# Gated delta layer: heads two tiles earlier, gates as the fifth tile, and a recurrence and spreads in another form

## The reference, cut to what matters

```
proj = h @ w_in                       # 1024 x (4*1024 + 16)
qkv, z, beta_logit, a_logit = split(proj)
qkv = silu(causal_conv(qkv, w_conv))  # 4 taps
q = q * rsqrt(sum(q*q)) / sqrt(128);  k = k * rsqrt(sum(k*k))
beta = sigmoid(beta_logit);  g = -exp(a_log) * softplus(a_logit + dt_bias)
# per head, per chunk: L = strict(k_beta k^T * decay);  T = (I + L)^-1
# u = T v_beta;  w = T (k_beta exp(g));  qk = causal(q k^T * decay)
# scan over chunks:
v_new = u - w @ state
o = q_dec @ state + qk @ v_new
state = state * exp(g_last) + k_dec^T @ v_new
y = (rms_norm(o) * silu(z)) @ w_out
```

## Time and profile before

| | |
|---|---|
| runs | 2340.86, 2342.62, 2348.20 us |
| profiled execution | 2341.71 us, of which the span is 2339.90 us |
| mean granted TensorE clock | 0.966 |
| TensorE matmuls | 2211.8 us busy, 95% |
| VectorE / ScalarE / GpSimd | 1127.8 / 854.7 / 412.3 us (48 / 37 / 18%) |
| DMA | 182.12 MB, mean 78 GB/s |

### The profile page before, as it was taken

One profiled execution on the slowest core, in us unless ns is written; L12 is line 12 of the kernel. 1 busy time (PEld: TensorE's weight loads), 2 busy tenths in 40 slices (PEclk: granted clock), 3 DMA queues, 4 the chain that ended last, 5 costly groups with the idle time before them and its releaser, 6 DMA issues. The chain is left out here.

```text
span 2339.9 us, 29203 instructions
## 1 busy us (share of the span) xinstructions
PE 2211.8 (95%) x10830; PEld 1776.7 (76%) x10830; DVE 1127.8 (48%) x1805; ACT 854.7 (37%) x1405; POOL 412.3 (18%) x459
## 2 busy tenths in 40 slices
PE   7999999999889999998899999999999997899989
PEld 6888887666677888887788878886777886776657
DVE  5444324423436444324575543346565775655433
ACT  4322223443334322223432241135445753433453
POOL 2111003112423111001210010002100241014441
PEclk8999999999989999999999999999999996999999
DMA  4333333411022333331333256740242220233202
GB/s 135 116 93 96 95 97 84 95 45 55 19 72 72 108 97 94 97 94 50 109 90 99 72 91 97 101 72 1 72 119 74 68 58 10 73 86 73 48 18 70
DMA packets 359321, 182.12 MB, mean 78 GB/s; under 512 B 41925, under 2 KB 356014, under 8 KB 358830
## 3 DMA queue, kind: packets, MB, share of 16 engines
q1 hardware_dynamic: 359214, 180.69, 31.0%
HBM read 176.14 MB, written 4.52 MB: 77 GB/s over the span
## 5 line engine op out<-in xcount | busy, mean ns | idle before, releaser
L313 PE MATMUL ps<-xh,wh 128*128 128x512 f32 x1920 | 766.0, 399 | 10.8 <-DVE wl L280 4.2
L315 PE MATMUL ps<-xh,wl 128*128 128x512 f32 x1920 | 749.3, 390 | 0.0
L314 PE MATMUL ps<-xl,wh 128*128 128x512 f32 x1920 | 748.5, 390 | 0.0
L280 DVE TENSOR_TENSOR wl<-raw,wh 128x1024 fp32r<-128x1024 f32 x334 | 422.6, 1266 | 435.7 <-ACT wh L270 431.0
L270 ACT ACTIVATE wh<-raw 128x1024 fp32r<-128x1024 f32 x334 | 342.1, 1027 | 375.3 <-PE ps L315 332.1
L313 PEld LDWEIGHTS ps<-xh,wh 128*128 128x128 f32 x1920 | 360.9, 188 | 102.9 <-issue 22.2
L315 PEld LDWEIGHTS ps<-xh,wl 128*128 128x128 f32 x1920 | 360.7, 188 | 77.3
L314 PEld LDWEIGHTS ps<-xl,wh 128*128 128x128 f32 x1920 | 361.1, 188 | 73.0 <-issue 2.4
L458 PE MATMUL ps<-xh,wh 128*128 128x512 f32 x304 | 129.9, 427 | 25.4 <-ACT xh L393 15.6
L451 POOL TENSOR_TENSOR acc<-acc,sq 128x512 f32<-128x512 f32 x72 | 102.6, 1424 | 273.1 <-ACT sq L836 178.0
L313 PE MATMUL ps<-a_hi,wh 128*128 128x512 f32 x352 | 136.9, 389 | 0.0
(11 more groups left out here) (380 smaller groups left out, 2560.7 us busy)
## 6 DMA issues: line engine op xcount, KB each, us to landing
raw<-in_w_ffn_gate SPq DMA_DIRECT2D x44, 512.0 KB, 3.8
raw<-in_w_ffn_up SPq DMA_DIRECT2D x44, 512.0 KB, 3.8
raw<-in_w_ffn_down SPq DMA_DIRECT2D x32, 512.0 KB, 3.8
raw<-in_conv_w_in SPq DMA_DIRECT2D x32, 512.0 KB, 4.0
raw<-in_fox_w_in SPq DMA_DIRECT2D x32, 512.0 KB, 9.9
raw<-in_gdn_w_in SPq DMA_DIRECT2D x32, 512.0 KB, 4.1
raw<-in_w_in SPq DMA_DIRECT2D x24, 512.0 KB, 3.8
raw<-in_swa_w_in SPq DMA_DIRECT2D x32, 256.0 KB, 3.8
```

The source lines that it names most:

```text
L280: nc.vector.tensor_tensor(wl[s][:, 0:kb, :], raw[r][:, 0:kb, :], wh[s][:, 0:kb, :].bitcast(F32), ALU.subtract).then_inc(lo_done, 1)
L313: pe.matmul(o, wh[s][:, kb, :], x_hi, start=start, stop=False)
L314: pe.matmul(o, wh[s][:, kb, :], x_lo, start=False, stop=False)
L315: return pe.matmul(o, wl[s][:, kb, :], x_hi, start=False, stop=stop)
```

## The change: what it does

1. The gates' tile is the fifth (BA = 4). The small steps on the gates move with it, four tiles earlier; the sums of k are read in step 11 and the sums of q differ as in 3.
2. The wait before tiles 4 and 5 asks for the eviction of the tile whose bank is overwritten (three back), in every projection that has a `pe_amid`.
3. Heads start at tile 15. One turn stands after each of tiles 4 to 19. The turns of q go to bank 2, one head at a time, and VectorE reads each at the start of `dve_amid` (semaphore `q_sums`, steps 13 to 20). Bank 2 is also the one that the keys are turned into, so TensorE waits for `q_sums` before L2217 in tiles 15 to 20.
4. Values are turned five tiles behind (V_LAG = 5), tiles 20 to 27.
5. The inversion starts in step 25, with ten columns there, ten in step 26, eleven in step 27, and the two block transposes and the copy at the end of step 27. All eight z tiles are evicted by ScalarE and GpSimd. ScalarE's three block copies stand in its step 32, after the eviction of tile 32.
6. In the recurrence, TensorE's order is: k times state, inverse times rest, q times state, state's products, scores times v_new, each for all four heads. VectorE copies the output of chunk t-1 between the rest and the state updates of chunk t, and the state update no longer waits for L2469.
7. Spreads are transposes, four records in place of eight.

```diff
-                if k == H8:
+                if k == 4:
...
-                m = pe.matmul(ps[STAT][:, t * P:t * P + P], rcol[:, t:t + 1].broadcast_to([P, P]), ident[:, :],
-                              start=True, stop=True)
+                m = pe.transpose(ps[STAT][:, t * P:t * P + P], rcol[:, t:t + 1].broadcast_to([P, P]), ident[:, :])
...
-                    wait(pe, evac, ev0 + o - (3 if amid is None or first_i else 1))
+                    wait(pe, evac, ev0 + o - (3 if amid is None or first_i or o in (4, 5) else 1))
...
-            K0, Z0, Z_POOL = 2 * H8 + 1, 3 * H8 + 1, 3 * H8 + 3
+            BA, K0, V_LAG, Z0 = 4, 2 * H8 - 1, 5, 3 * H8 + 1
...
             def pe_amid(pe, k, b):
...
+                        if k - 5 < 2 * H8:
+                            pe.wait_ge(q_sums, k - 4 - H8)
                         for t in range(TB):
                             ins = pe.transpose(blk(ps[2], t), blk(G[:, 8 + m, :], t), ident[:, :])
...
             def dve_amid(dve, k):
                 s = k - K0
+                if H8 <= k - 5 < 2 * H8:
+                    dve.wait_ge(g_ss, k - 4)
+                    nc.vector.tensor_scalar(nrm[:, 1, :, k - 5 - H8:k - 4 - H8], ps[2][:, 0:TB].rearrange("p (t o) -> p t o", o=1),
+                                            EPS, None, ALU.add).then_inc(q_sums, 1)
+                if k == Z0:
+                    g_tap(dve, k // 4, k % 4, 3)
...
-                if k == Z_POOL + 2:
+                if k == Z0 + 2:
                     substitute(dve, 20, B5 - 1)
+                    nc.vector.transpose(t11[:, :, 0:B5].rearrange("p n c -> p c n"),
+                                        ti[:, :, :].rearrange("p i c -> p c i")).then_inc(t11_d, 1)
+                    nc.vector.transpose(tt[:, :, 0:B5].rearrange("p n i -> p i n"), ti[:, :, :]).then_inc(tt_c, 1)
+                    dve.wait_ge(tt_c, 1)
+                    nc.vector.tensor_copy(tt[96:128, :, 96:128], tt[96:128, :, 0:32]).then_inc(tt_a, 1)
...
+                        for r in range(NR if t else 0):
+                            m = NR * rd + r
+                            pe.wait_ge(o_tok, at(rd, t - 1, r))
+                            pe.wait_ge(qd_p, m + 1)
+                            pe.matmul(ps[4 + r][:, 0:P], blk(G[:, m, :], t), blk(state, r), start=True, stop=False)
```

More of the change, by code:

```diff
@@ L2252, in pe_beside @@
                     m.then_inc(g_turned, 1)
-                for turn in ([k - 4] if 4 <= k < 4 + H8 else []) + ([H8 + k - 11] if 11 <= k < 11 + H8 else []):
+                turn = k - 4
+                if 0 <= turn < 2 * H8:
                     pe.wait_ge(g_sq, turn + 1)
@@ L2256, in pe_beside @@
                         pe.wait_ge(evac, ev0 + HEAD + 1)
[L2257 removed]
+                    bank, at_, apart = (ps[3], turn, H8) if turn < H8 else (ps[2], 0, 1)
+                    if turn > H8:
+                        pe.wait_ge(q_sums, turn - H8)
+                    if k >= K0:
+                        pe.wait_ge(tok_d, k - K0 + 1)
                     for t in range(TB):
[L2259 removed]
+                        m = pe.matmul(bank[:, t * apart + at_:t * apart + at_ + 1], X[:, 11 + turn % 2, t * P:t * P + P], ones[:, 0:1],
                                       start=True, stop=True)
                     m.then_inc(g_ss, 1)
[L2262 removed]
+                if k == BA + 5:
                     pe.wait_ge(g_al, 3)
@@ L2455, in pe_tail @@
                                       start=True, stop=True).then_inc(v_mm, 1)
+                        for r in range(NR if t else 0):
[3 more added lines that the diff above has]
+                            pe.matmul(ps[4 + r][:, 0:P], blk(G[:, m, :], t), blk(state, r), start=True, stop=False)
+                        for r in range(NR if t < TB - 1 else 0):
+                            pe.wait_ge(vn_d, at(rd, t, r))
+                            if t == 0:
+                                pe.wait_ge(*((back_a, 2 * H8 + 2 * rd + r + 1) if r < 2 else (tok_d, H8 + 2 * rd + r - 1)))
+                            pe.matmul(ps[r][:, 2 * P:3 * P], kdec(r, t), blk(vnew, r), start=True, stop=True).then_inc(s_mm, 1)
                         for r in range(NR):
@@ L2493, in dve_tail @@
                         ins.then_inc(tok_d, 1)
-                    for t in range(TB):
-                        for r in range(NR if t else 0):
+                    for t in range(TB + 1):
+                        for r in range(NR if 0 < t < TB else 0):
                             m = NR * rd + r
@@ L2499, in dve_tail @@
                                                            in1=blk(G[:, 16 + m, :], t), op0=ALU.mult, op1=ALU.subtract).then_inc(r_d, 1)
+                        for r in range(NR if t else 0):
+                            m = NR * rd + r
+                            dve.wait_ge(o_mm, at(rd, t - 1, r))
+                            nc.vector.tensor_copy(blk(G[:, m, :], t - 1), ps[4 + r][:, 0:P]).then_inc(o_tok, 1)
                         for r in range(NR if t < TB - 1 else 0):
```

121 lines of the change are left out of this document (49 added, 72 removed).

## The result

The changed kernel takes 2352.78 us (median of 20 executions, 2346.87 to 2356.68), the kernel before in the same rounds 2347.26 (2340.86 to 2354.82): a ratio of 1.0022, with a 95% interval of 1.0012 to 1.0032. That is a real loss, smaller than the 0.3% that I took as the bound of "no change", and inside the range. The profiled execution of the changed kernel took 2347.31 us with a span of 2345.6, against 2341.71 and 2339.9 before. So the two profiles differ by 5.7 us.

What follows compares the result with a forecast made beforehand. TensorE was taken as the bound where projections run, so an edit pays only by taking records or waits off it. 10.2 + 1.7 + 2.0 - 0.5 - 4.7 - 6.7 - 0.5 = +1.5 us gave 2344 us, range 2329 to 2357.

Steps and rivals of the forecast that it cites:

- no change: Whole kernel: a time between 2335.6 and 2349.6 us, within about 0.3% or 7 us; chance 0.46.
- the sum: Whole kernel: all terms together give +1.5 us, 2344 us; by itself from 2337 to 2351, chance 0.50.
- The new waits in tiles 15 to 20: Gated delta layer: TensorE waits before L2217 for VectorE's q_sums, 13.5 us in all.
- The first rival: Tiles 15 to 20: the new waits don't bite, since VectorE runs further ahead than 4.5 us; 2329 us, chance 0.17.
- The inversion: Gated delta layer: starts 2.9 us earlier, but late splits put the levels 52.6 us after its start, 10.2 us later.
- The second rival: Inversion: the late splits don't bite, it ends two tiles earlier and its idle time vanishes; 2320 us, chance 0.08.
- Levels: Behind the inversion: second level starts 5.3 us after the first instead of 5.8; gain 0.5 us, up to 3.
- Recurrence: Gated delta layer's recurrence: a step takes 4.6 us instead of 5.50; gain 4.7 us, bounds 3 and 5.5.
- Spreads: Eleven spreads and L1585: four transposes take 0.60 us against 1.05 for eight records; gain 6.7 us, bounds 3 and 8.
- Up to tile 15: Gated delta layer before tile 15: gains of 3.0 us at tile 4, 2.71 after tile 12 and 0.3.
- The clock: Waits of tiles 15 to 20 and tile 31: half clock follows, each costing 1.7 us; 2352 us, chance 0.25.
- the waits of tiles 4 and 5: Eviction waits: 3.0 us gained at tile 4 of the gated delta layer, 0.5 of 0.94 at tile 4 of mix_in.

Runs made afterwards that it cites:

- e1: The changed kernel with VectorE's read of each q sum moved to the end of the previous step, behind the eviction; ratio to before 0.9956, 2335.5 us.
- e2: The changed kernel with the inversion's columns cut into five parts over steps 25 to 29 instead of three over 25 to 27; ratio to before 0.9977, 2339.6 us.
- e5: The kernel before with the recurrence's new order alone, on TensorE and VectorE; ratio to before 0.9986, 2342.3 us.
- e10: The changed kernel with the spreads as products again instead of transposes; ratio to before 1.0077, 2361.6 us.
- e6: The kernel before with only the eviction wait of output tiles 4 and 5 loosened; ratio to before 1.0002, 2345.4 us.
- e4: The kernel before with only the spreads turned into transposes; ratio to before 0.9995, 2345.4 us.
- e3: The changed kernel with both q sums read a step earlier and the inversion in five parts; ratio to before 0.9915, 2326.1 us.
- e9: The kernel of e3 with the spreads as products again instead of transposes; ratio to before 0.9933, 2330.7 us.
- e7: The kernel of e3 with the keys' sums in bank 7 in place of bank 3; ratio to before 0.9895, 2320.4 us.
- e8: The kernel of e7 with VectorE's first-level eviction ahead of splits and ScalarE's third block copy and last two silus behind its own eviction; ratio to before 0.9881, 2316.4 us.

## Why the prediction was right

The forecast was no change, with 2344 as the likeliest time; the ratio puts the changed kernel 5 us above before where I had 1.4. Of the 8.8 us between 2344 and 2352.78, 4.6 are the kernel before's own (2347.26 in the shared rounds, 2342.62 when I wrote); the rest is the sum's. The waits and the recurrence came as forecast, the late splits with 9.1 us of idle time where I had 12.5; that the sum as a whole lands as near as it does is in part luck, as the points show:

- **The new waits in tiles 15 to 20** were the main term against the change: 13.5 us forecast, 12.15 in the trace, each with the releaser named. The first rival, that they don't bite, falls by the trace and by e1. The read stands 4.3 to 4.7 us behind the eviction (4.5 forecast).
- **The inversion**: levels 52.6 us after its start forecast, 52.5 measured, and that agreement is luck. VectorE has tile 31's split ready after 39.1 us, 1.8 sooner than I had, and half clock on tile 31 gives 1.7 back; the 52.6 had no half clock in them, I had added 1.7 for it apart. TensorE idled 4.51 us in tile 27 and 4.54 before tile 31, where I had 5.4 and 7.1. The second rival falls, by e2's 12.4 us between the two instants.
- **Levels**: the second starts 5.5 us after the first (1966.12 and 1960.63), forecast 5.3; the gain is 0.3 where I had 0.5.
- **Recurrence**: a step of 4.6 forecast, 4.61 measured. 4.7 us forecast, 5.4 in the trace, 3.8 ± 1.0 by e5 at an equal clock. **Spreads**: 6.7 forecast, 5.3 to 5.9 measured three times; this term was some 1 us too large. The prediction's "two times" counts the records; in time the factor is 1.05 over 0.60, 1.75.
- **Up to tile 15** is the step that fell short. I had 6.0 us for it, 3.0 of them at tile 4. The first turn does come 3.3 us sooner (35.45 after the layer's start, 38.73 before), but half clock stands behind it, and the second turn comes at 45.45, before at 45.13: nothing is left. The prediction named this cost at half its size ("1.5 if half clock now falls on tile 5"); it is 3.1 us (45.45 against e1's 42.34 behind an equal wait). With the 2.71 us gained and this given back, the turn ahead of tile 15 stands 2.5 us later than I had it.
- **The clock** was a rival of its own, at 0.25 and 2352 us, and the median, 2352.78, is its number and not mine. Of the seven waits that it names (the six in tiles 15 to 20 and the one at tile 31), two are followed by half clock in the profiled execution (1831 and 1947; 0.58 in the first window), and so is the wait of tile 27 (1920), which it does not name. From three on it claims the loss, so by its own count it stands at its edge. And this execution, 2347.31 at 0.964, is the second fastest of the twenty (mean clock 0.9626); how many such falls the median one had, no trace shows. The same six waits in e2 are followed by half clock once (1847), in e10 three times (1803, 1814 and 1851). So this rival is not excluded: at the mean clocks, 0.9626 against 0.9648, the slope gives it 3.4 us of the loss beside the 3.6 that remain at an equal clock.
- **Half clock elsewhere.** What I did not see is that it can come in a stage that the change does not touch: at the first wait of the next layer (sliding window) the changed kernel is 1.9 us behind (2102.18 against 2100.25 before, 3.27 us idle in both), the clock falls there and not before, and it is 4.7 behind at 2128.14 against 2123.46. By e5 and e6 this is not the change's doing: the profiled execution of the kernel before was lucky there (see e4), as it was behind its 2.71 us wait (see e5), the row from which I took only 2 us of clock for all six new waits.

So +1.5 stands against the profile's +5.7 like this. From the layer's start to the inversion I had -2.9, 0.45 less for a spread and 2.0 of clock, measured +2.8: 4.2 more. From the inversion's start to the first level I had 13.1 and 1.7 of clock, measured 13.0 with its clock in it: 1.8 less. Recurrence 0.7 better, the start of the program 7.7 ahead instead of some 6, levels 0.2 less gained. And behind the gated delta layer 3.3 lost, where I had 0.45 gained by the last spread.

At an equal clock the sum was too favourable: without its 3.7 us of clock it says -2.2, measured +3.6 ± 0.8. Spreads (1.4), recurrence (0.9) and the waits of tiles 4 and 5 (2.4 measured, 3.5 forecast) are 3.4 of these 5.8; the rest isn't located. Spreads, recurrence and the waits of tiles 4 and 5 are worth 5.3, 3.8 and 2.4 us, 11.5 in all; the kernel with all of the change and without its two faults (e3) stands at -20.3. If the gains add up, the new order of heads, gates and z tiles is worth the other 8.8, which no run has alone. The two faults cost 24.0, and the change ends at +3.6. So the change was not without effect: it held 20 us of gain and 24 of loss, and the loss came from where two short pieces stand on VectorE. What stays open is what decides whether a wait of 2.5 to 3.3 us is followed by half clock. The runs show that it happens with the same instructions either way (e5), and that the mean clock does not follow the transposes (e9, e10), and not more.

## What to carry to other kernels

When a buffer is reused sooner, count from the releasing engine's queue what stands ahead of the release: a read of 0.16 us behind an eviction, three taps and a split held TensorE for 12 us, and moving it to just behind that eviction cost nothing that the times show. Cut long runs on an engine that also feeds the bottleneck by the feeding's due times, not by their own count: five parts in place of three were worth 11 us. Where gains of a few us are sought, compare kernels at an equal granted clock, or a real saving (spreads, 5.3 us) reads as nothing, and 5.7 us between two medians (e7) are 1.5 ± 1.9. And a place where one profiled execution keeps its clock says little about the next one: look at the same wait in several executions before putting a price on it.

## What the runs showed of the hardware

- The same wait, before the same instructions, is followed by full or by half clock: 2.71 us with 1.00 and with 0.57 behind it, 2.50 with 1.00 and 0.66, 3.27 with 1.00 and 0.56. Over the profiled executions that have the wait, some half clock stands behind 2.55 us in three of twelve, behind 2.50 in four of seven, behind 2.71 in three of four and behind 3.27 in eleven of twelve. A wait of 0.85 us at the place of the 2.50 (e7, e8) was followed by 1.00 both times.
- Over 157 executions one thousandth of mean granted clock goes with 1.54 us, and one kernel's mean clock ranges over 0.961 to 0.969; that alone is 12 us.
- A transpose of a 128x128 f32 block by a broadcast column leaves one record of 272 ns at the median where the product leaves two, so that a spread of four takes 0.60 us in place of 1.05. By the factor of four that the Trainium skill (TensorE: Matmul & The Clock Gate, Terms) gives for FP32, four blocks would take about 0.3, an estimate; the trace does not agree, its factor is 1.75.
